# Two halves of the tokens for the late products of three transformer blocks and for the woven products behind them

## The reference, cut to what matters

```python
# first block
x = x + g1 * (y @ w_out)
h2 = modulate(rmsnorm(x, norm2_g), sh2, sc2)
x = x + g2 * ((silu(h2 @ w_gate) * (h2 @ w_up)) @ w_down)
# layers l = 0, 1
h = rms_norm(x, ln_mix_pre[l]);  proj = h @ w_in[l]
...
x = x + rms_norm(merged @ w_out[l], ln_mix_post[l])
h = rms_norm(x, ln_ffn_pre[l])
f = (silu(h @ ffn_w_gate[l]) * (h @ ffn_w_up[l])) @ ffn_w_down[l]
x = x + rms_norm(f, ln_ffn_post[l])
```

## Time and profile before

| | us, or as said |
|---|---|
| median of three runs | 3174.49 |
| the profiled execution | 3182.13 |
| its span, first to last instruction | 3180.3 |
| TensorE busy / VectorE / GpSimd / ScalarE | 2973.9 / 1426.4 / 1232.8 / 1201.9 |
| loads of the one hardware queue, of them 429 weight blocks | 81696 packets, 262.29 MB |
| mean granted clock of TensorE | 0.96 |

### The profile page before, as it was taken

The page is one execution under the profiler, slowest core; times in us unless marked ns, Lnnn a source line. Parts: engine busy times, 40 slices in busy tenths (PEclk is TensorE's granted clock), DMA queues, the critical chain, the costliest instruction groups (busy, mean ns, idle before and its releaser), DMA issues.

```text
span 3180.3 us, 33588 instructions
## 1 busy us (share of the span) xinstructions
PE 2973.9 (94%) x13120; PEld 2317.3 (73%) x13120; DVE 1426.4 (45%) x1895; ACT 1201.9 (38%) x1737; POOL 1232.8 (39%) x571
## 2 busy tenths in 40 slices
PE   6889899989999899999998999989898999989997
PEld 2777677768888666678776888866576877868886
DVE  5655642351111498852634302258977344161123
ACT  4226653233223455242334422244633333342222
POOL 3212122434444444344344444433533534444442
PEclk8888899999999999999999999989999999999998
DMA  5232212222222210122122222221011222222221
GB/s 205 100 103 91 89 63 74 80 88 100 97 96 97 75 47 27 60 73 97 69 86 78 95 100 94 99 72 60 8 60 60 100 77 82 95 76 98 97 100 60
DMA packets 81854, 264.44 MB, mean 83 GB/s; under 512 B 9216, under 2 KB 9344, under 8 KB 81696
## 3 DMA queue, kind: packets, MB, share of 16 engines
q1 hardware_dynamic: 81696, 262.29, 24.2%
HBM read 260.16 MB, written 2.10 MB: 82 GB/s over the span
## 4 chain that ended last, share of the span: by engine, by line
PE 75%; DVE 18%; ACT 4%; issue 1%; DMA 1%; POOL 0%; SPq 0%; ACTq 0%; DVEq 0%; POOLq 0%
PE bank L1344 22%; PE bank L1345 21%; PE bank L1346 21%; DVE pageF L2226 4%; PE bank L1547 2%; PE bank L1389 1%; DVE pageF L2017 1%; PE bank L1499 1%; DVE smal L2008 1%; DVE pageF L2303 1%; DVE pageF L2299 1%; PE bank L1376 1%; PE bank L1522 1%; DVE pageF L2034 1%; PE bank L1359 1%
## 5 line engine op out<-in xcount | busy, mean ns | idle before, releaser
L2335 POOL TENSOR_TENSOR wlo<-wraw,whi 128x1024 fp32r<-128x1024 f32 x429 | 1043.5, 2435 | 1667.8 <-ACT whi L1574 1662.7
L1344 PE MATMUL bank<-pageR,whi 128*128 128x512 f32 x3552 | 1446.7, 407 | 90.8 <-ACT pageR L1729 27.3
L1345 PE MATMUL bank<-pageR,whi 128*128 128x512 f32 x3552 | 1390.1, 391 | 0.0
L1346 PE MATMUL bank<-pageR,wlo 128*128 128x512 f32 x3552 | 1389.2, 391 | 0.0
L1344 PEld LDWEIGHTS bank<-pageR,whi 128*128 128x128 f32 x3552 | 679.9, 191 | 274.2 <-issue 113.0
L1345 PEld LDWEIGHTS bank<-pageR,whi 128*128 128x128 f32 x3552 | 680.8, 192 | 150.4 <-issue 20.8
L1346 PEld LDWEIGHTS bank<-pageR,wlo 128*128 128x128 f32 x3552 | 679.3, 191 | 141.4
L1574 ACT ACTIVATE whi<-wraw 128x1024 fp32r<-128x1024 f32 x429 | 450.7, 1053 | 407.4 <-PE bank L1346 404.2
L1613 ACT ACTIVATE pageR<-pageF 128x512 fp32r<-128x512 f32 x136 | 85.9, 632 | 435.9 <-DVE pageF L2094 208.3
L2226 DVE SCALAR_TENSOR_TENSOR pageF<-pageF,prm 128x497 f32<-128x497 f32 (+9 forms) x180 | 195.6, 1087 | 2.0
L1692 ACT ACTIVATE pageF<-bank,smal 128x512 f32<-128x512 f32 x96 | 65.9, 686 | 172.7 <-DVE smal L2008 172.5
(11 more groups left out here) (200 smaller groups left out, 2400.6 us busy)
## 6 DMA issues: line engine op xcount, KB each, us to landing
wraw<-in_wst SPq DMA_DIRECT2D x429, 512.0 KB, 3.4
pageF<-in_wmod SPq DMA_DIRECT2D x96, 256.0 KB, 4.8
pageF<-in_bias SPq DMA_DIRECT2D x16, 256.0 KB, 3.8
pageF<-in_xT SPq DMA_DIRECT2D x8, 256.0 KB, 6.9
out_x<-pageF SPq DMA_DIRECT2D x8, 256.0 KB, 2.0
pageF<-in_cT SPq DMA_DIRECT2D x4, 256.0 KB, 9.4
tabG<-in_tabG SPq DMA_DIRECT2D x1, 896.0 KB, 11.6
tabA<-in_tabA SPq DMA_DIRECT2D x1, 896.0 KB, 7.5
```

Of the source, the lines that this page charges most:

```text
L1344: e.matmul(o, hi, xh, start=first, stop=False)
L1345: e.matmul(o, hi, xl, start=False, stop=False)
L1346: i = e.matmul(o, lo, xh, start=False, stop=last)
L2335: e.tensor_tensor(wlo[:, b % NH, :, :], wraw[:, b % NR, :, :], bc(whi[:, b % NH, :, :]), ALU.subtract).then_inc(*wlod.up(("wlo", b)))
```

## The change

Every late product is made for tokens 0 to 255 first and then for tokens 256 to 511 (`late_halves`). Within a half it runs over two groups of four output pages; within a group the k loop is outside and the four pages inside, each in a bank of its own, so that a weight tile is used with 256 columns and is loaded, split and read twice, once for each half. Evictions, squares, `Squares`, `rstd`, `post_norm`, `in_hi`, `in_lo`, `in_sum`, `h2_hi`, `h2_lo`, `x_add`, `ffn_sum` and `store` take a half t of 256 columns (a page keeps its two halves side by side). `late_feeds` plans the norm of half 0 between the first tiles of half 1 of the late product; the norm of half 1 is planned between the first tiles of the woven products. These (`wide_halves`) run over all k for half 0, then over all k for half 1, in the same four banks. `Input.rms` makes its statistics twice, once for each half. The first woven group of the kernel (`wide`, with context) stays as it was, and so does the first half of k of ffn_down (`main_ffn`), whose loop is now left to its caller for the second half.

```diff
-NB = 429
+NB = 506
...
+    def wide_halves(self, items, xs, feeds):
+        outs = [self.mb.take(("o", name, m)) for name, m in items]
+        for t in range(2):
+            feed = iter(feeds[t])
+            for k in range(8):
+                for (name, m), o in zip(items, outs):
+                    s = self.w_next((name, m, k))
+                    self.step("mm", s, ((o, xs[k], t, 256 * t),), k == 0, k == 7)
+                    next(feed, None)
+                    yield
+            run(feed)
+
+    def late_halves(self, name, kts, xs, on_out):
+        for t in range(2):
+            for g in range(2):
+                ms = range(4 * g, 4 * g + 4)
+                outs = [self.mb.take(("oh", name, m, t)) for m in ms]
+                for i, k in enumerate(kts):
+                    for m, o in zip(ms, outs):
+                        s = self.w_next((name, m, k))
+                        self.step("mm", s, ((o, xs[i], t, 0),), i == 0, i == len(kts) - 1)
+                        yield t
+                for m, o in zip(ms, outs):
+                    on_out(m, t, o)
+                    yield t
...
+def late_feeds(late, norm):
+    first = norm(0)
+    for t in late:
+        if t:
+            next(first, None)
+    run(first)
+    return norm(1), ()
...
-    def norm_x2():
-        r = sq.rstd(1024, "ones", sbk, warm=True)
+    def norm_x2(t):
+        yield from pause(4)
+        sq[t].product("ones", sbk, True)
+        yield
+        r = sq[t].rstd(1024, "ones", sbk, True)
...
+                step("h2_hi", k, t)
             if k > 0:
-                step("h2_lo", k - 1)
...
+                step("h2_lo", k - 1, t)
...
+    def down_late(sfx, hs, on_half):
+        yield from p.late_halves("ffn_down" + sfx, range(FH, 2 * FH), hs, on_half)
...
         def rms(self):
-            sq = Squares(p, ("in", self.gain))
-            sq.n = 8
-            sq.rstd(1024, "ones", sbk)
+            for t in range(2):
+                sq = Squares(p, ("in", self.gain), half=t)
+                sq.n = 8
+                sq.rstd(1024, "ones", sbk)
...
+    def out_x_half(m, t, o):
+        step("x_add", o, m, 24, (("X2a", m),), ("X2", m), t)
+        mb.give(o, ("X2", m, t))
+        v0.hi(m, t)
...
+        def out_mix(m, t, o):
+            if t == 0:
+                pages.take(("F", l, m))
+            sf[t].add(o, 0, o, 0.5, m == 7)
+            step("evict_half", ("F", l, m), o, t)
+            mb.give(o, ("F", l, m, t))
...
         def post_norm(sf, f, done, gain, prev, ver, each):
-            r = sf.rstd(1024, "ones", mb, warm=True)
-            for m in range(8):
-                step("post_norm", (f, l, m), (done, l, m), gain, prev, r, m, (*ver, m))
-                pages.give((f, l, m), (*ver, m))
-                each(m)
...
+            def half(t):
+                yield from pause(4)
+                sf[t].product("ones", sbk, True)
                 yield
+                r = sf[t].rstd(1024, "ones", sbk, True)
+                for m in range(8):
+                    step("post_norm", (f, l, m), (done, l, m, t), gain, prev, r, m, (*ver, m), t)
...
+                    each(m, t)
+                    yield
...
+        def out_f_half(m, t, o):
+            step("ffn_sum", l, m, o, t)
+            mb.give(o, ("F2s", l, m, t))
+            sf2[t].add(("F2", l, m), 256 * t, ("F2s", l, m, t), last=m == 7)
...
-                    w.wait_ge(*when(*x, "hi"))
-                    w.wait_ge(*when(*x, "lo"))
+                    if t is None:
+                        w.wait_ge(*when(*x, "hi"))
+                        w.wait_ge(*when(*x, "lo"))
+                    else:
+                        xh, xl, o = xh[:, 256 * t:256 * t + 256], xl[:, 256 * t:256 * t + 256], o[:, c:c + 256]
+                        w.wait_ge(*when(*x, "hi", t))
+                        w.wait_ge(*when(*x, "lo", t))
                     e.matmul(o, hi, xh, start=first, stop=False)
                     e.matmul(o, hi, xl, start=False, stop=False)
                     i = e.matmul(o, lo, xh, start=False, stop=last)
```

More of the change, by code:

```diff
@@ L186, in linear @@
             s = self.w_next((name, m, k))
-            self.step("mm", s, tuple((o, xs[i]) for o, xs in groups), i == 0, i == len(kts) - 1)
+            self.step("mm", s, tuple((o, xs[i], None, 0) for o, xs in groups), i == 0, i == len(kts) - 1)
             if i % every == every - 1:
@@ L315, in run, with yield_from @@
         pass
+def yield_from(gen):
+    while True:
+        try:
+            next(gen)
+        except StopIteration as end:
+            return end.value
+def late_feeds(late, norm):
[5 more added lines that the diff above has]
+    return norm(1), ()
 def planned():
@@ L773, in main_ffn @@
                 if j == 0:
-                    yield from p.wide([(n + sfx, i) for i in range(2) for n in ("ffn_gate", "ffn_up")],
-                                      xs, None, rs and rs.rms, feed)
+                    yield from p.wide_halves([(n + sfx, i) for i in range(2) for n in ("ffn_gate", "ffn_up")], xs,
+                                             feeds)
+                    if rs is not None:
+                        rs.rms()
                 if j >= 2:
@@ L1139, in layer @@
-        vf = Input("ffn_pre" + L, ("X3", l))
-        feed = post_norm(sf, "F", "F", "mix_post" + L, rs.gain, ("X3", l), vf.hi)
-        sf2 = Squares(p, ("ffnp", l))
-        def out_f(hf, m, o):
-            if hf == 0:
-                evict(("F2", l, m), o)
-            else:
-                step("ffn_sum", l, m, o)
-                mb.give(o, ("F2s", l, m))
-                sf2.add(("F2", l, m), 0, ("F2s", l, m), last=m == 7)
-        run(main_ffn(L, vf.xs, out_f, feed, vf))
-        if l == 0:
-            nxt = Input("mix_pre1", ("X4", 0))
-            return nxt, post_norm(sf2, "F2", "F2s", "ffn_post" + L, vf.gain, ("X4", 0), nxt.hi)
@@ L1155, in layer @@
-        run(post_norm(sf2, "F2", "F2s", "ffn_post" + L, vf.gain, ("X4", 1), lambda m: step("store", m)))
-    layer(1, *layer(0, v0, ()))
+        sf = [Squares(p, ("mixp", l), half=t) for t in range(2)]
+        def out_mix(m, t, o):
+            if t == 0:
+                pages.take(("F", l, m))
+            sf[t].add(o, 0, o, 0.5, m == 7)
+            step("evict_half", ("F", l, m), o, t)
+            mb.give(o, ("F", l, m, t))
+        def post_norm(sf, f, done, gain, prev, ver, each):
+            def half(t):
+                yield from pause(4)
+                sf[t].product("ones", sbk, True)
+                yield
+                r = sf[t].rstd(1024, "ones", sbk, True)
+                for m in range(8):
+                    step("post_norm", (f, l, m), (done, l, m, t), gain, prev, r, m, (*ver, m), t)
+                    if t:
+                        pages.give((f, l, m), (*ver, m, t))
+                    each(m, t)
+                    yield
+                if t:
+                    pages.give(r, (*ver, 7, 1))
+            return half
@@ new lines, in layer, with out_f @@
+        vf = Input("ffn_pre" + L, ("X3", l))
+        feeds = late_feeds(p.late_halves("w_out" + L, range(8), M, out_mix),
+                           post_norm(sf, "F", "F", "mix_post" + L, rs.gain, ("X3", l), vf.hi))
+        p.drop(M, ("oh", "w_out" + L, 7, 1))
+        sf2 = [Squares(p, ("ffnp", l), half=t) for t in range(2)]
+        def out_f(m, o):
+            evict(("F2", l, m), o)
+        def out_f_half(m, t, o):
+            step("ffn_sum", l, m, o, t)
+            mb.give(o, ("F2s", l, m, t))
+            sf2[t].add(("F2", l, m), 256 * t, ("F2s", l, m, t), last=m == 7)
@@ new lines, in layer @@
+        hs = yield_from(main_ffn(L, vf.xs, out_f, feeds, vf))
+        nxt = Input("mix_pre1", ("X4", 0))
+        if l == 0:
+            return nxt, late_feeds(down_late(L, hs, out_f_half),
+                                   post_norm(sf2, "F2", "F2s", "ffn_post" + L, vf.gain, ("X4", 0), nxt.hi))
+        last = late_feeds(down_late(L, hs, out_f_half),
+                          post_norm(sf2, "F2", "F2s", "ffn_post" + L, vf.gain, ("X4", 1),
+                                    lambda m, t: step("store", m, t)))
@@ L1158, in planned @@
+        run(last[0])
+    layer(1, *layer(0, v0, ((), ())))
     assert len(p.order) == 8 * NB, len(p.order) / 8
@@ L1336, in mm @@
                 w.wait_ge(*when("wlo", b))
-                for n, (name, x) in enumerate(groups):
-                    if first:
+                for n, (name, x, t, c) in enumerate(groups):
+                    if first and not (t and c):
                         clear(name)
```

277 lines of the change are left out of this document (142 added, 135 removed).

## The result

The changed kernel takes 3327.43 us (median of four runs, 3325.96 to 3329.95), the kernel before, beside it, 3175.99: a ratio of 1.0477 [1.0459, 1.0495], 151 us slower. The profiled execution has a span of 3325.8 us against 3180.3: +145.5.

A forecast was written before the change was run, and what follows sets the result against it. TensorE, busy 94%, was taken as the bound: one matmul stream plus holes at stage seams. Seam costs and 5.5 us of longer stream gave +99, collisions +19: +118 on the 3174.49 median, 3292.5 us, range 3205 to 3365.

The forecast's parts named there:

- The stream: Late and woven products: 616 tiles at half width, matmuls 0.115 us apart, each tile 0.009 us dearer: +5.5 us.
- Group switches: Between groups of four pages in late products, TensorE waits for banks to empty: +3.2, +2 or +2.5 us each.
- Low clock: TensorE's clock stays low after a hole; two new holes at each of four stage seams with post-norms: +4 a seam.
- The norm of half 0 behind half 1: In half 1 of late products, weight splits or evictions wait behind half 0's norm: +13 to +16 us before switches.
- Seam 6: After layer 1's ffn_down, to the end: three switches 9.6 us and a shorter tail, 7.4 in all, plus up to 8 collisions.
- Statistics: Made twice behind the woven products: +4 us each after ffn_down of the first block and layer 0, elsewhere covered.
- Collisions: In norm passes, VectorE steps are slowed beside GpSimd splits and sums: 43 us if all paid, +19 taken.
- The rule on weight loads: Skill's rule: loads overlap products only where row groups differ, so 1848 more loads add an estimated 197 us; prediction doubted it.
- rival (d): Weight loads set the pace of half matmuls at 0.19 us: +277, 3570 us; chance 0.04.
- (a): Faster: queues keep up, weight splits behind the norm come before step 40 of half 1: about -30, 3145 us; chance 0.11.
- (c): GpSimd's weight splits, held back by VectorE, set the pace of all half blocks: +68 more, 3360 us; chance 0.09.
- (e): Halves run but the norm is first used after half 1, so seams stay: +50 to +80 us; no separate chance.

The follow-up runs named there:

- columns_cut: Kernel before the change, with 456 late tiles made as six matmuls of 256 columns instead of three of 512, same weights and order: 3196.65 us, ratio 1.0058.
- weights_twice: Kernel before the change, with late products run page by page once per token half, weights loaded and split twice, norms whole: 3196.53 us, ratio 1.0059.
- late_halves_only: Changed kernel with late products page by page, woven products at full width again and half 1's norm planned otherwise: 3231.22 us, ratio 1.0167.
- page_by_page: Changed kernel with late products run one page after another within each half, k inside, instead of groups of four: 3255.17 us, ratio 1.0241.
- late_spread: Changed kernel with half 0's norm, after five pieces, planned one piece every fifth step of half 1: 3318.12 us, ratio 1.0444.
- woven_spread: Changed kernel with half 1's norm, after five pieces, planned one piece every third step of the woven products: 3325.03 us, ratio 1.0468.
- norm_after_group: Changed kernel with half 0's norm, but its first five pieces, planned from half 1's second group on, every third step: 3322.98 us, ratio 1.0456.

## Why the prediction was right, and what was mis-sized

It said slower, 3292.5 with a range to 3365; it came to 3327.43, +151 instead of +118. The mechanism was right in the main, and its parts missed by more than the total did. By its steps:

- **The stream.** Right in kind, mis-sized: "say 0.115" a half matmul came from runs of three between full ones. Between themselves they are 0.1196 apart, so a tile costs 0.037 more and not 0.009: 616 tiles +22.5 us instead of +5.5. columns_cut shows it without anything else of the change. By the prediction's own list of what would make it wrong, half matmuls that aren't 0.115 apart, this one came true.
- **77 more loads and splits cost nothing by themselves.** Right; weights_twice shows it for 57. That a split's slack halves counts where the norm holds ScalarE, and at seam 6 where stores hold the loads.
- **Group switches**, 3.2, 2 and 2.5 us each. The idle time was near: at the switch behind half 0 of seam 4 waits of 1.15, 0.68 and 0.68, at seam 2 8.9 us in all against 4x2.5, though there the two longest stand behind collisions, which the sum prices elsewhere. For w_out of a layer it was too much: no wait over 0.4 us at the switches of half 0 of seam 3, instead of 2. What failed is that no low clock was counted behind them.
- **Low clock**, "+4 a seam" at four seams. Those 16 us are new low clock, while some 11 us of the old one lie in the stretches that the prediction subtracts, so net it forecast about 5; some 30 came. I had priced it only behind the two norm waits of a seam. Seam 2 has no such wait, and its clock column falls from 1.00 to 0.93: some 7 us behind its switches alone; seam 6 from 1.00 to 0.88, some 6.
- **The norm of half 0 behind half 1.** Right in place and engine: the stalls stand in the middle of each half 1, ended by the low weights of L2444 or by an eviction, with ScalarE in the norm. Right in size, nearly: ScalarE is free 25.3 us after half 0's last matmul (2141.06 to 2166.38), forecast 22.3; products go on after 29.0, forecast 25.9; half 1's last matmul starts at 2195.95, 54.9 after, forecast 45.7. The extra comes from the collision at the next switch (4.00 us where 3.2 were forecast for the whole switch), from later waits and from the clock.
- **Seam 6.** Forecast 7.4, and up to 8 of collisions; it became 24.1. The prediction counted three switches and the tail, and nothing for half 0's norm under half 1. It cost 10.1 us of idle time (2.75 and 7.33), the longer part through stores ahead of the weight loads: the late load that the prediction says would stall TensorE one for one, but for which it had no cause. With the pages in turn the seam has one wait of 3.4 us. No run changes the place of the stores alone.
- **The woven group**, -6.4 at seam 4 and -4.5 at 3. At 3 it held: from the first squares' product behind half 1 (1788.69) to 1823.30 are 34.6 against 38.7. At 4 it did not: 2197.38 to 2236.28 are 38.9, and 40.3 from the last late matmul, against 40.6. Switch waits, a 7.74 us stall and the clock ate it. late_halves_only shows that this group with its halves and their plan costs 24 us in all, once the late product goes page by page.
- **Statistics**, +4 at seams 2 and 4: 2.3 each in the wait. Elsewhere they were to be covered; behind seam 1 the wait grew by 2.7, and behind seams 3 and 5 stands a new one of 2.0 whose cause the profile doesn't show. Merging them brought 2.6 us for all seams, which can't be told from nothing.
- **Collisions**, +19 of up to 43: the rows show them (2.58, 2.14 us). Without the sums 15 us went, their own time included; what post_norm and in_lo pay wasn't tried alone, so no run shows what the collisions cost in all. Forecast idle time, with collisions, was 99 - 5.5 - 16 + 19 = 96 (tail and statistics in it), or 107 with the 11 us of old low clock that it had subtracted; measured 78 - 3.5 + 4.6 = 79, and 86 with the new waits behind seams 1, 3 and 5. So idle time was some 21 us too high, low clock some 25 and the stream 17 too low, and some 10 of busy time at the stops weren't counted at all. That they cancel in part is luck, and 118 comes as near to 151 as it does by it. The `in_lo` of the earlier trace rows ended 0.5 us behind the split, not with it.
- **The rule on weight loads** (Trainium skill, "TensorE: Matmul & The Clock Gate", sections "The mechanism" and "LDWEIGHTS (loading the stationary operand)"). columns_cut answers it: 1368 more matmuls, each with its load, added 18.5 us, and their loads still overlap them. The trace's side was the right one, and rival (d) is out. By the rule those loads would have added an estimated 146 us at 107 ns each. The section "The mechanism" of the Trainium skill also lets a load into a background weight buffer run ahead of matmuls in flight, which the prediction left out; the runs fit that and don't show which buffer was used.
- **Rivals.** (a) needed the norm pass to end by 14 us; it ended at 25. (c), GpSimd as the pace: weights_twice speaks against it, and seam 2 of page_by_page runs at full pace with GpSimd busy for 78.93 of 86.27 us. It is close, though. (e): the halves do what they say; the 9 us holes are gone.

**What was argued and then fell.** After the result I held that the queue order makes the loss, and that another plan would give it back. Three plans (late_spread, woven_spread, norm_after_group) gave 9, 2 and 4 us, the last two hardly to be told from nothing. The wait moves: spread the norm, and it is `x_add`, `ffn_sum` or `evict_half` that stands behind a piece of it; move it behind group 0, and group 1's evictions do. Two causes are shown: four pages that end together where there are only four banks (72 us, nearly all at the seams where VectorE empties the banks), and halves as such (53 us left in late_halves_only, with 456 of the tiles; of these 18.5 are pace). That the remaining 35 are the norm chain run twice, some 21 us of ScalarE and VectorE (2145.45 to 2166.38, weight splits between) that the product's other half can't hide, fits the waits but wasn't isolated. No version here beats the kernel before; the best is 50 us slower.

## What to carry to other kernels

Halving tokens to overlap a norm with a product pays only if the helpers' queues have room for the whole norm, twice, beside the weights' own work; price that chain against the half product before anything else. Using all banks in one group made every group's end a stop where the emptying of a bank shared an engine with other steps (4.3 us each at seam 2), and hardly where ScalarE emptied them alone (2.9 us at a whole seam). Stops also brought low clock, some 30 us beside 78 of idle time here, so count the stops, not only their microseconds. Look what stands ahead of the weight loads in the queue that issues them. And take a matmul's spacing from a run of its own width, not from a few among wider ones.

## What was not expected of the hardware

- Half-width matmuls cost 0.1196 us among themselves and about 0.115 between full ones: twice 0.1196 is 0.239 against 0.227, by these two widths an estimated 0.012 us that each matmul costs whatever its width.
- The granted clock stood at 0.50 for a while even behind a group switch with 2.2 us of idle time (1028 to 1035.5), and at 1.00 throughout where TensorE never stopped (seam 2 of page_by_page). Matmuls at 0.50 are some 30 of the 145.5 us, by the estimate above.
- A two-input VectorE step of 0.42 us took 2.58 and 2.14 beside a GpSimd split, and ended 0.3 us behind it both times.
